# A chunked recurrence: state product in an own PSUM bank, loads one per chain step, a Horner factor, and the second unit of a round half a round later

## The reference, cut to what matters

```python
def step(state, inp):
    r_t, w_t, k_t, v_t, kk_t, a_t = inp
    sa = jnp.einsum('bhvk,bhk->bhv', state, -kk_t)
    state = (state * w_t[:, :, None, :]
             + sa[..., None] * (kk_t * a_t)[:, :, None, :]
             + v_t[..., None] * k_t[:, :, None, :])
    return state, jnp.einsum('bhvk,bhk->bhv', state, r_t)
...
_, y = lax.scan(step, s0, tuple(map(seq_first, (r, decay, k, v, kk, a))))
mean = jnp.mean(y, axis=-1, keepdims=True)
var = jnp.mean(jnp.square(y - mean), axis=-1, keepdims=True)
yn = ((y - mean) * lax.rsqrt(var + RWKV_GN_EPS)).reshape(bsz, length, RWKV_WIDTH)
```

## Time and profile before

| what | value |
|---|---|
| median of 3 timed runs | 2832.94 us (2831.69 to 2835.86) |
| the profiled execution's own time | 2827.87 us |
| its span, first to last instruction | 2826.1 us |
| granted TensorE clock, mean | 0.966 |
| TensorE busy (matmul) | 2584.2 us, 91% of the span |
| VectorE, ScalarE, GpSimd busy | 1571.1, 1313.0 and 321.0 us |
| the stage of the recurrence | from 1212.5 to 1809 us |

### The profile page before, as it was taken

How to read it: one execution, slowest core, us unless ns; L and a number is a source line. 1 busy time by engine, 2 the same in 40 slices (tenths; PEclk the granted TensorE clock), 3 DMA queues, 4 the chain that set the end, 5 groups by cost and what they waited for, 6 DMA issues and landing times. The chain is left out here.

```text
span 2826.1 us, 64905 instructions
## 1 busy us (share of the span) xinstructions
PE 2584.2 (91%) x27593; PEld 2153.8 (76%) x27593; DVE 1571.1 (56%) x2294; ACT 1313.0 (46%) x2199; POOL 321.0 (11%) x367
## 2 busy tenths in 40 slices
PE   6999999999989999979888999799895999999992
PEld 5989886777766666778888888678784788888882
DVE  4566664442045555534344444553325888888885
ACT  5555542222134444324444444552222777777771
POOL 0121222331000000001212121200000000000002
PEclk9999999999999999989999999899996999999996
DMA  4443432212123224140202000144255999999976
GB/s 108 159 170 122 144 147 81 94 61 79 40 96 93 64 85 157 36 129 5 96 18 96 18 21 18 39 134 127 85 216 195 370 395 396 391 399 394 396 309 254
DMA packets 160693, 440.46 MB, mean 156 GB/s; under 512 B 14343, under 2 KB 94873, under 8 KB 148145
## 3 DMA queue, kind: packets, MB, share of 16 engines
q1 hardware_dynamic: 144461, 381.94, 37.6%
q10 hardware_dynamic: 9060, 29.56, 2.8%
q0 software_dynamic: 6912, 25.17, 2.3%
HBM read 344.22 MB, written 92.41 MB: 154 GB/s over the span
## 5 line engine op out<-in xcount | busy, mean ns | idle before, releaser
L2591 DVE TENSOR_TENSOR ex_wL<-wx,ex_wH 128x2048 fp32r<-128x2048 f32 x192 | 436.1, 2286 | 46.3 <-ACT ex_wH L2495 44.5
L2495 ACT CAST ex_wH<-wx 128x2048 fp32r<-128x2048 f32 x192 | 366.4, 1912 | 93.8 <-PE ex_bank L2391 70.6
L2389 PE MATMUL ex_bank<-ex_wH,ex_xTH 128*128 128x512 f32 x512 | 200.0, 391 | 2.4 <-DVE ex_xTL L2596 2.4
L2391 PE MATMUL ex_bank<-ex_wL,ex_xTH 128*128 128x512 f32 x512 | 199.8, 390 | 0.0
L2390 PE MATMUL ex_bank<-ex_wH,ex_xTL 128*128 128x512 f32 x512 | 199.7, 390 | 0.0
L709 PE MATMUL ph_acc<-ph_wH,uH 128*104 128x512 f32 x480 | 192.5, 401 | 6.5 <-DVE ph_wL L721 6.5
L709 PE MATMUL ph_acc<-ph_wH,uL 128*104 128x512 f32 x480 | 189.5, 395 | 0.0
L709 PE MATMUL ph_acc<-ph_wL,uH 128*104 128x512 f32 x480 | 189.5, 395 | 0.0
L413 PE MATMUL pf_acc<-uH,pf_wH 128*128 128x348 f32 x648 | 160.5, 356 | 6.3 <-DVE pf_wL L533 6.3
L413 PE MATMUL pf_acc<-uL,pf_wH 128*128 128x348 f32 x648 | 138.6, 322 | 0.0
L413 PE MATMUL pf_acc<-uH,pf_wL 128*128 128x348 f32 x648 | 138.3, 322 | 0.0
(11 more groups left out here) (397 smaller groups left out, 6623.7 us busy)
## 6 DMA issues: line engine op xcount, KB each, us to landing
wx<-in_expert_w_gate SPq DMA_DIRECT2D x32, 2048.0 KB
wx<-in_expert_w_up SPq DMA_DIRECT2D x32, 2048.0 KB
wx<-in_expert_w_down SPq DMA_DIRECT2D x32, 2048.0 KB
s_y<-ex_y ACTq DMA_DIRECT2D x32, 512.0 KB, 10.1
fw<-in_w_in SPq DMA_DIRECT2D x27, 512.0 KB
hw<-in_w_in SPq DMA_DIRECT2D x6, 2048.0 KB, 10.1
s_qkT<-ph_stg ACTq DMA_DIRECT2D x4, 2080.0 KB, 6.9
mb_gt<-s_pT SPq DMA_DIRECT2D x16, 512.0 KB, 3.5
```

The costliest lines, as they stand in the source:

```text
L2389: nc.tensor.matmul(out, aH, bH, start=first, stop=False)
L2391: return nc.tensor.matmul(out, aH, bL, start=False, stop=last)
L2495: nc.scalar.copy(wH[:, w, part], raw(j, s)[:, part]).then_inc(w_high, 1)
L2591: nc.vector.tensor_tensor(wL[:, w, part], raw(j, s)[:, part], wH[:, w, part], ALU.subtract).then_inc(w_low, 1)
```

## The change

Nine edits, all in `rwkv`:

- The product of piece 4 goes to bank 1; the `m` work has bank 0 alone. The semaphore `seq_add` and TensorE's wait for it before piece 5 are gone.
- ScalarE multiplies the old state by the decay (`SP`, two instructions after R); VectorE makes the new state by two `scalar_tensor_tensor` of half width, product times decay plus `SP`, and waits for `decayed`.
- `load(d)` becomes `load(d, n)`, n = 0 to 9, each after one more chunk; the order of SP's queue changes, and `load_branch` comes last.
- Steps 10 to 12 make I + Y(I + Y(I + Y)) with one orientation of Y copied (`Y1`), and all three adds read PSUM.
- The first solve unit of a round (A) keeps its round; the second (B) starts half a round later, and its steps 9 to 12 fall into the next round.
- The halves `m` of the chunk ahead move to other places in the round.
- `Q0` is made by GpSimd as soon as `M4` is there, with four buffers.
- The first clearing of PSUM is divided otherwise between VectorE and ScalarE.
- TensorE's first use of the solve banks waits for ScalarE's clearing.

```diff
-        STEPS = {"pe": (2, 6, 7, 8, 9, 10, 11, 12), "dve": (2, 7, 8, 9, 11, 12),
-                 "act": (6, 7, 8, 10, 11), "pool": (6,)}
+        STEPS = {"pe": (2, 6, 7, 8, 9, 10, 11, 12), "dve": (2, 7, 8, 9, 10, 11, 12),
+                 "act": (6, 7, 8, 10), "pool": (6,)}
...
-            step = lambda n: [("solve", ch, n) for ch in (A, B)] if new else []
+            first = lambda n: [("solve", A, n)] if new else []
+            second = lambda n: [("solve", B, n)] if new else []
+            late = lambda n: [("solve", B - 2, n)] if old else []
             tokens = lambda ch: [("tok", ch)] if new else []
             ahead = lambda ch, e: [("m", ch, e)] if new and nxt else []
             piece = lambda: [("seq",) + next(pieces)] if old else []
-            return (step(2) + tokens(A) + piece() + step(6) + piece() + tokens(B) + step(7) + piece() + step(8) + piece() + piece()
-                    + step(9) + ahead(A + 2, 0) + piece() + step(10) + ahead(A + 2, 1) + piece() + step(11) + ahead(B + 2, 0) + piece()
-                    + step(12) + ahead(B + 2, 1) + piece() + piece())
+            return (first(2) + late(9) + tokens(A) + piece()
+                    + first(6) + late(10) + ahead(A + 2, 0) + piece()
+                    + first(7) + late(11) + ahead(A + 2, 1) + piece()
+                    + first(8) + late(12) + piece() + piece()
+                    + first(9) + second(2) + tokens(B) + piece()
+                    + second(6) + first(10) + ahead(B + 2, 0) + piece()
+                    + first(11) + second(7) + ahead(B + 2, 1) + piece()
+                    + first(12) + second(8) + piece() + piece())
...
-            def load(d):
+            def load(d, n):
                 z = d % 2
-                if d >= 2:
-                    sp.wait_ge(seq_pe, seq_done(NCH * (d - 1) - 1, 5))
-                for e in range(2):
-                    for dst, j in ((BK[z][:, e, 0], BHAT), (KR[z][:, e, 0], KAP), (KR[z][:, e, 1], RHAT), (BK[z][:, e, 1], KHAT),
-                                   (V[z][:, e], VAL)):
-                        sp.dma_start(dst, c.rwD[2 * d + e, j]).then_inc(x_in[z], 16)
+                e, k = divmod(n, 5)
+                dst, j = ((BK[z][:, e, 0], BHAT), (KR[z][:, e, 0], KAP), (KR[z][:, e, 1], RHAT), (BK[z][:, e, 1], KHAT), (V[z][:, e], VAL))[k]
+                if d > 1 or n > 0:
+                    sp.wait_ge(seq_pe, seq_done(NCH * (d - 1) - 1 + n, 5))
+                sp.dma_start(dst, c.rwD[2 * d + e, j]).then_inc(x_in[z], 16)
...
-            load(1)
+            load_rest(0)
+            for gi in range(1, 2 * ND):
+                if gi % 2 == 1 and gi // 2 + 1 < ND:
+                    for n in range(10):
+                        load(gi // 2 + 1, n)
+                load_rest(gi)
             for i in range(2):
                 load_branch(sp, c, c.w_branch_rwkv, c.bw[:, i], i, early_in)
-            load_rest(0)
-            load_rest(1)
-            for gi in range(2, 2 * ND):
-                if gi % 2 == 0 and gi // 2 + 1 < ND:
-                    load(gi // 2 + 1)
-                load_rest(gi)
...
-                    if ch > 1:
-                        pe.wait_ge(m_read, ch - 1 + OPEN)
+                    if ch > 0:
+                        pe.wait_ge(m_read, ch + OPEN)
                 for j in range(2):
                     for h in range(2):
-                        last = mm(bank[here(h), ch % 2, (4 * e + 2 * j) * TC:(4 * e + 2 * j + 2) * TC].rearrange("p (a t) -> p a t", a=2),
+                        last = mm(bank[here(h), 0, (4 * e + 2 * j) * TC:(4 * e + 2 * j + 2) * TC].rearrange("p (a t) -> p a t", a=2),
...
-                            mm(at(bx, 0, e, h), Nn[here(h), ln, 1, e, :], Qf[here(h), f, e, :], start=True, stop=True)
+                            mm(at(bx, 0, e, h), Qf[here(h), f, e, :], Nn[here(h), ln, 1, e, :], start=True, stop=True)
                         for h in range(2):
-                            last = mm(at(bx, 1, e, h), Qf[here(h), f, e, :], Nn[here(h), ln, 1, e, :], start=True, stop=True)
+                            last = mm(at(bq, 0, e, h), Nn[here(h), ln, 1, e, :], Qf[here(h), f, e, :], start=True, stop=True)
                 elif n == 11:
                     pe.wait_ge(*at_act(ch, 10))
+                    pe.wait_ge(*at_dve(ch, 10))
                     for e, h in PAIRS:
-                        last = mm(at(bx, 0, e, h), Y1[here(h), ln, 0, e, :], Y1[here(h), ln, 1, e, :], start=True, stop=True)
+                        last = mm(at(bx, 0, e, h), Y1[here(h), ln, e, :], G[here(h), ln, e, :], start=True, stop=True)
...
-                    pe.wait_ge(*at_act(ch, 11))
                     pe.wait_ge(*at_dve(ch, 11))
                     for e, h in PAIRS:
-                        last = mm(at(bq, 0, e, h), Y2[here(h), ln, e, :], G[here(h), ln, e, :], start=True, stop=True)
+                        last = mm(at(bq, 0, e, h), Y1[here(h), ln, e, :], G[here(h), ln, e, :], start=True, stop=True)
...
-                            mm(bank[half(h), 6, 384 + RD * e:384 + RD * e + RD], tok[here(h), s, 0, e, :], Uu[here(h), e, :], start=True, stop=False)
+                            mm(bank[half(h), 1, RD * e:RD * e + RD], tok[here(h), s, 0, e, :], Uu[here(h), e, :], start=True, stop=False)
                         for h in range(2):
-                            last = mm(bank[half(h), 6, 384 + RD * e:384 + RD * e + RD], tok[here(h), s, 1, e, :], vv(e, h), start=False, stop=True)
+                            last = mm(bank[half(h), 1, RD * e:RD * e + RD], tok[here(h), s, 1, e, :], vv(e, h), start=False, stop=True)
                 else:
-                    if t < NCH - 1:
-                        pe.wait_ge(seq_add, added(ch))
...
+                    if 0 < t < NCH - 1:
+                        act.wait_ge(seq_dve, added(ch - 1))
+                        for e in range(2):
+                            last = nc.scalar.mul(SP[:, e], S[:, t % 2, e], c.Pend[:, 2 * d + e, t:t + 1])
+                        last.then_inc(decayed, 1)
...
-            nc.scalar.mul(bank[:, 6:8, :], c.eps[:].unsqueeze(2).to_broadcast([128, 2, 512]), 0.0).then_inc(tok_emptied, 1)
+            zero = lambda b, n: nc.scalar.mul(bank[:, b, 0:n], c.eps[:].to_broadcast([128, n]), 0.0)
+            for b, n in ((2, 4 * TC), (3, 2 * TC), (4, 4 * TC), (5, 2 * TC)):
+                last = zero(b, n)
+            last.then_inc(emptied_act, 1)
...
-            def solve(ch, n):
+            def masked(ch, e):
                 ln = ch % 2
                 eye = maskn[0:PX, 2].unsqueeze(1).to_broadcast([PX, 2, TC])
-                if n == 6:
+                if e == 1:
                     pool.wait_ge(m_read, ch + 1 + OPEN)
-                    if ch >= 2:
-                        pool.wait_ge(*at_dve(ch - 2, 9))
-                    nc.gpsimd.tensor_tensor(Q[0:PX, ln, 0], M4[0:PX, ch % MS, :, 0, :], eye, ALU.add).then_inc(spool[ln], 1)
+                    if ch >= TS4:
+                        pool.wait_ge(*at_dve(ch - TS4, 7))
+                    nc.gpsimd.tensor_tensor(Q0[0:PX, ch % TS4], M4[0:PX, ch % MS, :, 0, :], eye, ALU.add).then_inc(spool[ln], 1)
...
-                if n == 11:
-                    dve.wait_ge(*at_act(ch, 10))
-                    tt(G[0:PX, ln], Y1[0:PX, ln, 0], maskn[0:PX, 2].unsqueeze(1).to_broadcast([PX, 2, TC]),
-                       ALU.add).then_inc(sdve[ln], 1)
+                if n >= 10:
+                    if n == 12 and ch >= TS4:
+                        dve.wait_ge(seq_pe, seq_done(ch - TS4, 3))
+                    tt(Gf[0:PX, ch % TS4] if n == 12 else G[0:PX, ln], pairs(bx if n == 11 else bq),
+                       maskn[0:PX, 2].unsqueeze(1).to_broadcast([PX, 2, TC]), ALU.add).then_inc(sdve[ln], 1)
...
-                    src = bank[:, 6, 384:512].rearrange("p (e d) -> p e d", e=2)
+                    src = bank[:, 1, 0:2 * RD].rearrange("p (e d) -> p e d", e=2)
                     dve.wait_ge(seq_pe, seq_done(ch, 4))
                     if t == 0:
-                        nc.vector.tensor_copy(St[:], src).then_inc(seq_add, 1)
+                        tt(S[:, 1], src, c.Pend[:, 2 * d:2 * d + 2, 0:1].to_broadcast([128, 2, RD]), ALU.mult).then_inc(seq_dve, 1)
                     else:
-                        dve.wait_ge(seq_dve, added(ch - 1))
-                        tt(St[:], src, S[:, t % 2], ALU.add).then_inc(seq_add, 1)
-                    dve.wait_ge(seq_add, added(ch))
-                    tt(S[:, (t + 1) % 2], St[:], c.Pend[:, 2 * d:2 * d + 2, t:t + 1].to_broadcast([128, 2, RD]), ALU.mult).then_inc(seq_dve, 1)
+                        dve.wait_ge(decayed, (NCH - 2) * d + t + OPEN)
+                        for e in range(2):
+                            last = nc.vector.scalar_tensor_tensor(out=S[:, (t + 1) % 2, e], in0=src[:, e], scalar=c.Pend[:, 2 * d + e, t:t + 1],
+                                                                  in1=SP[:, e], op0=ALU.mult, op1=ALU.add)
```

(4 more changed lines are left out.)

30 lines of the change are left out of this document (12 added, 18 removed).

## The result

The changed kernel takes 2795.53 us (median of 4 runs, 2791.34 to 2799.17) against 2832.32 us (2828.31 to 2835.86) for the kernel before on the same chip: a ratio of 0.987 [0.985, 0.989], 37 us or 1.3% faster. The forecast was 2758 us and 75 us of gain; the result lies at the upper edge of its range. The sign was right, the gain is half of what was forecast.

The account below looks back on a forecast made before the run. TensorE was taken to bound the recurrence stage, through stretches standing still or running slowly. Gains of 47 + 29 + 9 = 85 us less 10 given back made 75 us, so 2758 us, range 2738 to 2796.

Parts of the forecast that it names:

- 76 chain steps (4 x 19) x 0.63 = 48 us; I take 47: Own bank for the state product: piece 5 no longer waits for VectorE's add, saving 0.63 us per chain step.
- A clean round becomes 13.18 - 1.26 = 11.9 us: Recurrence stage: an undisturbed round shortens from 13.18 to 11.9 us once the wait before piece 5 goes.
- Loads one per chain step: Spreading each block's ten-load burst on SP's queue ends TensorE's stops there: 29 us gained, or 0 if any load stops it.
- the branch loads: Eight `w_branch_rwkv` loads moved behind the last group loads make a burst there: 3 us charged (0 to 7).
- no stops without releaser after single loads: Sign expected in the profile after: TensorE does not stand still unreleased behind single loads.
- bursts not cured: Rival: stops come with any load or have another reason, so 29 us stay: 2787 us, chance 0.07.
- Horner factor: Steps 10 to 12: adds reading PSUM replace slowed L1631, 6.5 us of waits plus about 2 for the clock: 9 us gained.
- Decayed state on ScalarE: Two 64-column multiplications in ScalarE's queue after R, 0.30 us each, holding up nothing queued behind them by their wait.
- The second unit half a round later: Solve order: no work added; most distances between a unit's steps are 0.8 to 1.9 us against 0.6 needed, two tight.
- tight distances: Between steps 10 and 11 of the first unit, and pieces 3 and 4: 2 us charged for the first, second met.
- a rival of 24: Each half round loses 0.3 us more than walked as two queues push each other along: 2782 us, chance 0.20.
- Bank 7: Second unit's tokens wait for evacuation of the group norm's third transposes: 0.8 us, in 7 groups 5 us; 1 more for second transposes.

Follow-up runs that it names:

- e9: The kernel before with the state product in bank 1, `m` in bank 0 alone and no wait for `seq_add`, no other edit: 2823.64 us, ratio 0.996.
- e1: The changed kernel with a wait for the new state put back before piece 5: 2825.57 us, ratio 0.9971 to the kernel before.
- e5: The kernel before with the change's loads alone, one per chain step and branch loads last: 2821.8 us, ratio 0.9963.
- e2: The changed kernel with a block's ten loads in one go again and the branch loads at the start: 2816.84 us, ratio 0.9946 to the kernel before.
- e4: The changed kernel with the round's order of before, both solve units in step: 2809.2 us, ratio 0.9929 to the kernel before.
- e7: The changed kernel with `m` products of 52 columns instead of 104, same instruction count: 2797.45 us, ratio 0.9877 to the kernel before.
- e8: The changed kernel with step 2 and half of step 10 writing 104 columns instead of 52, same instructions: 2805.85 us, ratio 0.9908 to the kernel before.
- e10: The changed kernel with step 7's two same-weight products merged, an implied step 6 wait dropped, one VectorE copy more: 2783.89 us, ratio 0.9826 to the kernel before.
- e6: The changed kernel with the group norms' four loads and eight branch loads also one per chain step: 2793.28 us, ratio 0.9854 to the kernel before.
- e11: The changed kernel with step 7's products merged, step 6's implied wait dropped and all stage loads one per chain step: 2783.45 us, ratio 0.982 to the kernel before.
- e3: The changed kernel with six already met waits added in each piece of TensorE's stream: 2840.57 us, ratio 1.0031 to the kernel before.

## Why the prediction was half right, step by step

**The step that failed** is the first: "76 chain steps (4 x 19) x 0.63 = 48 us; I take 47", and with it "A clean round becomes 13.18 - 1.26 = 11.9 us". The term measured 12 us alone (e9) and 30 when undone in the changed kernel (e1). The step took TensorE's standing still as the only price of the wait. The gap was really closed (0.12 us instead of 0.74), the new state was never late (no wait of piece 1 for it), and one round does run in 12.11 us. But the wait also had a use: it gave the instruction fetch time. The short stops for code rose from some 6 to 33.7 us, and the wait put back, 58 us in all, took 28 us of stops out (e1). In e9 some 8 us more went to the one bank left for `m`, which the prediction charged with 1 us, at the start. The evidence had been in hand: I had read "TensorE ran out of code" in the bursts and took that as a matter of the bursts. The step that I left out is to ask how far the supply is from its limit in quiet parts: 5 packets in 16 us is a packet per 3.2 us there (4.35 over the stage), and a stream 10% faster needs them 10% sooner.

**Loads one per chain step.** "Together 29", less 3 for the branch loads. Measured: 10 alone (e5), 21 when undone in the changed kernel (e2). The mechanism was right: stops above 2.3 us hardly occur, and the windows at the block boundaries went from 42.1 and 38.8 us per 1000 matmuls to about 32. What failed is "no stops without releaser after single loads": they are smaller but everywhere. The rival "bursts not cured" (nothing gained) falls, though e5 lies nearer to it than to the 26. The Trainium skill (SBUF - State Buffer, SBUF: two separate sides) says that a DMA and a compute operation can't slow each other; e2 against the changed kernel has the same operations with other loads and 21 us between them. That doesn't contradict the rule for data in SBUF, but a kernel whose code is fetched by DMA has this path beside it. The branch loads made two stops, 0.90 and 1.95 us, as charged (3).

**Horner factor.** "L1631 is gone ... 9 us." All 240 adds take 254 to 269 ns, beside GpSimd's gate too:

```profile
L1643 DVE TENSOR_TENSOR rw_G<-rw_bank,maskn x160: 265/267/269, 1223.4 to 1766.5; 116x104 f32<-116x104 f32 x160
```

The 6.5 us of waits for L1631 don't appear in the waits after, and the half clock from 1225 us on went from 42.8 to 3.4 us. This edit wasn't run alone, so its share is open. Subtraction gives an idea: the changed kernel with the old order (e4) is 24 us faster than before, of which own bank and loads alone bring 12 and 10; that leaves about 2, if they added up, which e1 and e2 say they don't. The sum's 9 us for this term are not shown.

**Decayed state on ScalarE.** I took 0.30 us for a multiplication; it takes 0.34.

```profile
L1535 ACT ACTIVATE rw_SP<-rw_S,Pend x144: 334/338/340, 1234.9 to 1765.5; 128x64 f32<-128x64 f32 x144
```

The Trainium skill (ScalarE: Activation LUTs, What ACT_TABLE_LOAD costs) gives 0.33 us by its price per column and pointer, and the trace agrees with it, not with my interpolation. It cost nothing that can be seen: waits for `rw_X` and `rw_Y` sum to about 1 us in the stage.

**The second unit half a round later.** I charged 2 us for tight distances and had a rival of 24 (chance 0.20). The tight distances hold: step 11 starts 0.08 us behind the record before it instead of some 0.05, some 1.5 us in all where 2 were charged; e7 shows how little was to spare. And the order is worth 14 us (e4), some 8 of it because the old order makes `m` wait for its one bank, 7 to 10 by the clock. That lay outside every case I had.

**Bank 7.** "0.8 us, in 7 groups 5 us": there are 7 such waits, 2.4 us in all, so 0.3 to 0.4 each.

So the small charges were right within some 4 us, as far as rows show them, and the order was better than charged by some 20 us. The two large gains, booked at 47 and 26, brought 12 and 10 alone and cost 30 and 21 undone, so they neither add up nor reach their face value. For the first the runs show why: half of the removed wait comes back as stops for code. That the result still lies just inside the range owes something to luck: the two terms were 22 to 51 us too large together, and the order, charged as a loss, made up for part of it.

## What to carry to other kernels

In a stage of many tiny instructions, ask of each wait that you remove what else goes on behind it; where the trace shows stops that nothing released, and they follow packets of the instruction queue, price the stage in instructions too, and test it by changing column time at the same instruction count (e7, e8) before you plan on TensorE's busy time, and look whether the edit uncovers a hand-over. Here, merging two products with the same weights into a wider one and dropping a wait that is implied (e10) gave more than a shorter matmul. Spread large loads, but one load of half a megabyte per chain step is enough; finer spreading gave nothing (e6, e11).

## What the runs showed of the hardware

- TensorE's code came in packets of 16 KB, one per 256 of its instructions (35,014 to 137). In the changed kernel a packet came every 4.09 us on average, and 56 of 57 stops without a releaser ended 2.1 to 3.0 us behind a packet's start. That the packets are the cause rests on these times and on e1, e8 and e10; no run delays a packet by itself.
- Half clock (0.50) costs 0.37 of its time here: 23 matmuls per us against 36. Stops spaced through the stage brought up to 34 us of it (e2, e5), the changed kernel had 3.4.
- 26 us of column time less, at the same instruction count, changed the time by nothing that can be measured, though some 6 us of it went to waits for a copy (e7); 26 us more cost 10 (e8); 17 instructions of 438 less, with 3 us of column time, brought 15 us (e10).
- A wait instruction that was already met cost some 38 ns in TensorE's queue (45 us for 1200, e3), its share of the code included; in a row they start 0.11 us apart.
- With the products `m` of both chunks in one bank, TensorE waited for the mask 35 times, each start 0.054 or 0.055 us behind its end (e4, e9).
- An add with one operand in PSUM and one in SBUF keeps its 267 ns beside a GpSimd operation; one with both in SBUF took 2.4 us for two.
